# Two-block transformer kernel: sums of squares of the input through a buffer per tile, input scaled by 1/rms ahead of the last modulation columns

## The chip, the cores and the metric

The kernel runs on 1 core of one Trainium2 chip. The metric is the device time of one execution in microseconds; three runs of the kernel before took 3841.53, 3845.0 and 3848.81 us, median 3845.0 us.

## What is computed

The reference is a chain of two diffusion-style blocks (gated linear attention, then neighbourhood attention, each with a convolutional feed-forward part) and two further blocks, all in float32 with D = 1024, 512 latent tokens and 256 context tokens. The change touches only its very beginning: the first normalisation and modulation, whose result `h` goes into the product with `gla_w_in`.

```python
def rms_norm(x, g):
    y = xf * lax.rsqrt(jnp.mean(xf * xf, axis=-1, keepdims=True) + EPS)
    return y * g
def modulate(x, g, shift, scale):
    return rms_norm(x, g) * (1 + scale) + shift

mod_l = silu(c) @ ada_w[0] + ada_b[0]          # 6 parts of 1024; the same for the context with c_ctx
h_l = modulate(x_lat, norm1_g[0], sh1_l, s1_l)
h_c = modulate(x_ctx, norm1_g[0], sh1_c, s1_c)
proj = concat(h_c, h_l) @ gla_w_in[0]
```

## The kernel before, in words

Activations lie transposed, features on the 128 partitions: `X` is 8 tiles (k = 0 to 7) of 768 columns, of which columns 0 to 255 are the context and 256 to 767 the latent tokens (`lat(X, k)`). The products with weights run as three fp32r matmuls (high x high, high x low, low x high): each factor is split in a rounded half (`AH`, `WHI`, written by ScalarE) and the rest (`AL`, `WLO`, written by VectorE). `high_half` (L1375) and `low_half` (L2104) split one 128x1024 piece of weights; three such pieces are held in `RAW`, and SP may load piece i only once the low half of piece i - 3 is made (`weights`, L2990).

Five programs, one for each engine, are written out by hand; every instruction that others need counts up its engine's semaphore under a name (`q.did(name)`), and `q.wait_ge(name)` waits for it. Each engine works through its own list in order. A name of the form `fence("end_norm0")` stands for the end of the start-up in all four compute engines.

The start-up is the part that the change rewrites. It does three things.

1. The modulation columns. The weights `ada_w` come in 512 KB pieces ("side" pieces, L2967), four to a group of 512 outputs; groups 0 to 3 are needed before the first normalisation. Piece m uses one of six slots, so piece m waits until `ada_chunk` of piece m - 6 has run on TensorE (`("amm", m - 6)`). `ada_chunk` (L719) is 8 small float32 matmuls. After four of them VectorE copies the row out (`ada_rows`, L2156), TensorE turns it by 4 tiny matmuls (`ada_turn`, L730) and VectorE adds the bias (`ada_add`, L2161). When group 3 is added, `scale_cols` (L2193) makes the factors (1 + scale) * g, named `acol`.
2. The sums of squares. For each k ScalarE squares the latent part into `SQ[0]` and the context part into `SQ[1]` (L1427); TensorE sums over the partitions by a product with ones into PSUM banks 6 and 7 (`square_sum`, L680). With one buffer each, square k + 1 waits for the sum of tile k. Where the eight pairs of sums stand among the chunks of `ada` is set by the table `STATS0_AT`: from the second chunk of group 1 to the third of group 3.
3. The norm. `norm_two` runs two generators side by side, latent and context. ScalarE's (`norm_high`) waits for the last sum and for `acol`, makes 1/rms with Ln (L1399) and Exp (L1402), and then per tile the rounded half with the shift added (L1411) from the VectorE result `ntr`; VectorE's (`norm_low`) makes `ntr = x * acol * rs` (L2134) and the low half `(ntr + shift) - high` (L2128). After tiles 0 and 1 one piece of weights is split on both engines (`between=(0, 1)`).

TensorE then starts `lin_pair` (L654): the first two 128-column jobs of `gla_w_in` together, tile by tile, 12 matmuls of 384 columns for each k, as the halves of that tile come. After that pair it takes the side piece 16 (`ada_chunk`), which SP may load only after `fence("end_norm0")`, as it may the table `lcs` ahead of it and, since they stand behind in SP's list, the weight pieces from number 3 on. SP's list at the start is: small tables; side 0 to 3; latent tiles 0 to 3 of x (1 MB); side 4, 5; the context (1 MB); side 6, 7; latent tiles 4 to 7 (1 MB); side 8 to 15; weight pieces 0 to 2.

Of the kernel before, what the change touches and what calls it, by code (L numbers as in the profile page):

```python
# [15 lines left out]
D = 1024  # L16
# [291 lines left out]
def build(nc, A, out):  # L308
# [17 lines left out]
    def at(name, shape, dt, off):  # L326
        return nc.alloc_sbuf_tensor_at(name, shape, dt, offset=BASE + int(off))

    def ring(name, n, off, shape=(128, TL), dt=F32):
        size = 4 * int(np.prod(shape[1:]))  # L330
        full = tuple(slice(None) for _ in shape)
        return [at(f"{name}{i}", list(shape), dt, off + size * i)[full] for i in range(n)]
# [63 lines left out]
        return [("modmm", i, cg - 1) if cg else ("modmm", 0, 11)]  # L396

    NORM = [(ring(f"nrs{b}_", 1, oV + 8 * KB * b), ring(f"ntr{b}_", 3, oV + 2 * KB + 8 * KB * b)) for b in range(2)]
    QK = at("gqk", [128, 4, 2, T0], F32, oX0)
    Qt, Kt = QK[:, :, 0, :], QK[:, :, 1, :]  # L400
    Vt = at("gv", [128, 6, D], F32, oV)
# [145 lines left out]
    U = Buf(UH, UL)  # L547
    RL = ring("rl", 3, oX0 + 80 * KB)

    STATS0_AT = ((1, 1), (1, 3), (2, 0), (2, 2), (2, 4), (3, 0), (3, 1), (3, 2))  # L550
    NA_ITEMS = [(j, i) for j in range(8) for i in range(4)]
    KIND = (0, 1, 1, 2)
    MLA_ITEMS = [(j, i) for j in range(4) for i in range(4)]
# [22 lines left out]
    def squares_of(h, s, e_):  # L576

        return SQO[(h, s) == (3, 1)][e_]

    def fence(name):  # L580
        return [(name, n) for n in ("pe", "act", "dve", "pool")]

# [2 lines left out]
    def pe_program(q):  # L585
# [122 lines left out]
        def ada_chunk(i, cg, g):  # L708

            m = next(side_count)  # L710
            b = cg % 2 if m < SIDE_IN else 6
            if g == 0:
                bank(b, ("rows", i, cg))
            p = PS[b]
            q.wait_ge(("aw", m), ("cs",))
            for k in range(2):
                for half in range(2):
                    at32, at2 = 64 * k + 32 * half, 2 * (2 * g + k)
                    mm = e.matmul(p[at32:at32 + 32, 0:256], CS[:, at2:at2 + 32], side_slot(m)[0][:, k, 256 * half:256 * half + 256],  # L719
                                  start=g == 0, stop=g == 3, skip_group_check=True)  # L720
# [12 lines left out]

        def ada(i, cg, mb_bank):
            for g in range(4):
                ada_chunk(i, cg, g)
                yield
            yield
            ada_turn(i, cg, mb_bank)
            yield  # L740

        def ada_beside(fill):

            for n, (i, cg) in enumerate(fill):
# [9 lines left out]
            for _ in range(n):  # L754
                next(side, None)

        k = 0
        for cg in range(4):
            for n, _ in enumerate(ada(0, cg, 2 + cg % 2)):
                if (cg, n) in STATS0_AT:  # L760
                    if k == 0:
                        bank(6, ("ln", "x", 0)), bank(7, ("ln", "x", 1))
                    square_sum("x", k, TL, PS[6], k == 0, k == 7, 0, 0)
                    square_sum("x", k, TC, PS[7], k == 0, k == 7, 1, 1)
                    k += 1
        q.note("end_norm0", "pe")


# [595 lines left out]
    def act_program(q):  # L1364
# [48 lines left out]
                    yield  # L1413
            yield

        def norm_two(N_, stats, i, n, mem, free, between=()):
            gens = [norm_high(N_ + v, stats, r, 8, lambda k, a=a, w=w: AH[:, k, a:a + w], mem[r],
                              free + [("acol", i, n)], bias=lambda k, r=r: mod(i, 3 * n, r, k), rbank=6 + r)
                    for r, (v, (a, w)) in enumerate((("l", SEGL), ("c", SEGC)))]
            for k, _ in enumerate(zip(*gens)):  # L1420
                if k in between:
                    high_half()

        def square(S, k, r, src, buf, *ready):
            q.wait_ge(*ready)
# [34 lines left out]
        e.activation(CS[:, 0:16].rearrange("p (k v) -> p v k", v=2), SMT[:, ca:ca + 16].rearrange("p (v k) -> p v k", v=2),  # L1460
                     ACT.Silu).then_inc(q.did("cs"))

        k = 0
        for cg in range(4):
            for n in range(6):
                if (cg, n) in STATS0_AT:
                    square("x", k, 0, lat(X, k), 0, *sq_by[0], ("x_lat", k // 4))
                    square("x", k, 1, X[:, k, 0:TC], 1, *sq_by[1], ("x_ctx",))
                    sq_by[:] = [[("sqmm", "x", k, 0)], [("sqmm", "x", k, 1)]]
                    k += 1  # L1470
        norm_two("g", "x", 0, 0, NORM, [], (0, 1))
        q.note("end_norm0", "act")


# [620 lines left out]
    def dve_program(q):  # L2095
# [43 lines left out]
            low(srcs - 1)  # L2139
            yield  # L2140

        def norm_two(N_, i, n, mem, free, ready, between=()):
            gens = [norm_low(N_ + v, None, 8, lambda k, a=a, w=w, r=r: (X[:, k, a:a + w], ready(k, r)),
                             lambda k, r=r: ACOL[:, i, n, r, k:k + 1],
                             lambda k, a=a, w=w: AH[:, k, a:a + w], lambda k, a=a, w=w: AL[:, k, a:a + w],
                             mem[r], free + [("acol", i, n)], bias=lambda k, r=r: mod(i, 3 * n, r, k))
                    for r, (v, (a, w)) in enumerate((("l", SEGL), ("c", SEGC)))]
            for k, _ in enumerate(zip(*gens)):
                if k in between:
                    low_half()  # L2150

# [6 lines left out]
        def ada_add(i, cg, b):  # L2158
# [3 lines left out]
                            PS[b][:, 0:8].rearrange("p (j h v) -> p h j v", h=2, v=2),  # L2162
                            SMT[:, ab:ab + 4].rearrange("p (h j) -> p h j", h=2).unsqueeze(3).to_broadcast([128, 2, 2, 2]),
                            ALU.add).then_inc(q.did("mod", i, cg))

        def ada(i, cg, mb_bank):
            for g in range(4):
                yield
            ada_rows(i, cg, cg % 2)
            yield  # L2170
            ada_add(i, cg, mb_bank)
            yield

        def ada_beside(fill):
            for n, (i, cg) in enumerate(fill):
# [20 lines left out]
        for cg in range(4):  # L2196
            for _ in ada(0, cg, 2 + cg % 2):
                pass
        scale_cols(0, 0)
        norm_two("g", 0, 0, NORM, [], lambda k, r: [("x_ctx",)] if r else [("x_lat", k // 4)], (0, 1))  # L2200
        q.note("end_norm0", "dve")


# [658 lines left out]
    def pool_program(q):  # L2862
# [6 lines left out]
                e.tensor_tensor(SQ[0], SQ[0], SQ[1], ALU.add).then_inc(q.did("sqacc", S, k))  # L2869

        e.memset(CS[:, :], 0.0).then_inc(q.did("cs_zero"))
        q.note("end_norm0", "pool")


# [75 lines left out]
    def sp_program(q):  # L2950
# [47 lines left out]
        load(SMT[:, 0:sm["_n"]], A["small"], "small")  # L2998
        load(FIX[:, :], A["fix"], "fix")
        load(SEL[:, :], A["sel"], "sel")  # L3000
        for _ in range(4):
            side()
        load(lat4(X, 0), XT[:, 0:4, :], "x_lat", 0)
        for _ in range(2):
            side()
        load(X[:, :, 0:TC], CTX, "x_ctx")
        for _ in range(2):
            side()
        load(lat4(X, 4), XT[:, 4:8, :], "x_lat", 1)
        for _ in range(8, 16):  # L3010
            side()
        weights(LOOK + 1)
        load(CG[:, :], A["cg"], "cg", after=[("modmm", 0, 2), ("modmm", 0, 3)])
# [174 lines left out]
```

## Time and profile before

| what | value |
|---|---|
| median of three runs | 3845.0 us |
| the profiled execution, its own time | 3843.47 us |
| its span, first to last instruction | 3841.7 us |
| TensorE busy | 97% of the span |
| VectorE, ScalarE, GpSimd busy | 41%, 36%, 6% |
| mean granted TensorE clock | 0.990 |

The page gives busy times over the whole span; the start-up is 2% of it, so it is read from the timeline and from busy times of short stretches instead. All times in those views count from the first instruction of the span.

### The profile page before, as it was taken

How to read it: one execution, taken by the hardware profiler on the slowest of the kernel's cores; microseconds unless marked ns; L12 is line 12 of the kernel's file. 1: busy time of each engine (PE TensorE's matmuls, PEld its weight loads, DVE VectorE, ACT ScalarE, POOL GpSimd, SP SyncE). 2: the span in 40 equal slices, each digit the busy share in tenths (PEclk: the TensorE clock that was granted, in tenths of full speed). 3: DMA queues.
4: the chain of work that ended last, by engine and by line, in shares of the span. 5: the costliest groups of instructions: out<-in, count | busy, mean ns of one | idle time of the engine just before them, and what ended most of it. 6: DMA issues, size and time to landing. Idle time of an engine off the chain costs nothing.

```text
span 3841.7 us, 45535 instructions
## 1 busy us (share of the span) xinstructions
PE 3713.4 (97%) x19200; PEld 2993.6 (78%) x19200; DVE 1590.8 (41%) x2532; ACT 1389.0 (36%) x2257; POOL 233.7 (6%) x191
## 2 busy tenths in 40 slices
PE   7998899999999999999899999999999999999998
PEld 5887777888887977888666768888877676888887
DVE  3216735423434155545445443433334544343333
ACT  3235523212224255323346442342324544234232
POOL 0000010000000001000000001120110001012011
PEclk9999999999999999999999999999999999999999
DMA  6320022333322222233211123322221122332322
GB/s 225 110 88 2 28 83 88 112 122 130 110 64 83 66 69 77 94 93 96 89 57 50 66 72 99 104 93 99 94 93 57 54 71 71 96 105 93 99 93 83
DMA packets 108702, 333.98 MB, mean 87 GB/s; under 512 B 11473, under 2 KB 26705, under 8 KB 108369
## 3 DMA queue, kind: packets, MB, share of 16 engines
q1 hardware_dynamic: 108496, 331.06, 26.7%
q8 instruction: 151, 2.47, 0.3%
q14 instruction: 55, 0.44, 0.0%
HBM read 327.35 MB, written 2.10 MB: 86 GB/s over the span
## 4 chain that ended last, share of the span: by engine, by line
PE 92%; DVE 4%; ACT 2%; DMA 1%; issue 1%; POOL 0%; SPq 0%; DVEq 0%; ACTq 0%
PE ps L618 69%; PE ps L671 6%; PE ps L654 2%; PE ps L719 1%; PE ps L680 1%; PE ps L1213 1%; PE ps L1061 1%; PE ps L1049 1%; PE ps L1040 1%; PE ps L863 1%; PE ps L890 1%; DMA aw<-ada_d 1%; PE ps L1216 1%; PE ps L1092 1%; PE ps L1257 1%
## 5 line engine op out<-in xcount | busy, mean ns | idle before, releaser
L2104 DVE TENSOR_TENSOR wlo<-raw,whi 128x1024 fp32r<-128x1024 f32 (+3 forms) x547 | 618.9, 1132 | 888.2 <-ACT whi L1375 887.2
L1375 ACT ACTIVATE whi<-raw 128x1024 fp32r<-128x1024 f32 (+3 forms) x547 | 527.1, 965 | 795.0 <-PE ps L618 624.9
L618 PE MATMUL ps<-bh,whi 128*128 128x512 f32 x1248 | 494.7, 396 | 0.1
L618 PE MATMUL ps<-bh,wlo 128*128 128x512 f32 x1248 | 486.0, 389 | 0.0
L618 PE MATMUL ps<-bl,whi 128*128 128x512 f32 x1248 | 485.9, 389 | 0.0
L618 PE MATMUL ps<-ah,whi 128*128 128x512 f32 (+2 forms) x1424 | 423.3, 356 | 0.2 <-ACT gv L1500 0.2
L618 PE MATMUL ps<-al,whi 128*128 128x512 f32 (+2 forms) x1424 | 417.7, 352 | 0.0
L618 PE MATMUL ps<-ah,wlo 128*128 128x512 f32 (+2 forms) x1424 | 415.0, 350 | 0.0
L618 PEld LDWEIGHTS ps<-ah,whi 128*128 128x128 f32 x1424 | 240.0, 188 | 51.1 <-issue 18.8
L618 PEld LDWEIGHTS ps<-bh,whi 128*128 128x128 f32 x1248 | 234.2, 188 | 58.1 <-issue 7.6
L618 PEld LDWEIGHTS ps<-bl,whi 128*128 128x128 f32 x1248 | 234.4, 188 | 50.5 <-issue 2.9
L618 PEld LDWEIGHTS ps<-bh,wlo 128*128 128x128 f32 x1248 | 234.2, 188 | 49.3
L618 PEld LDWEIGHTS ps<-ah,wlo 128*128 128x128 f32 x1424 | 242.1, 188 | 31.5
L618 PEld LDWEIGHTS ps<-al,whi 128*128 128x128 f32 x1424 | 241.3, 188 | 29.4
L618 PE MATMUL ps<-uh,whi 128*128 128x512 f32 x512 | 199.2, 389 | 0.0
L618 PE MATMUL ps<-ul,whi 128*128 128x512 f32 x512 | 199.2, 389 | 0.0
L618 PE MATMUL ps<-uh,wlo 128*128 128x512 f32 x512 | 199.2, 389 | 0.0
L2869 POOL TENSOR_TENSOR sq<-sq,sq 128x512 f32<-128x512 f32 x50 | 77.0, 1540 | 1905.8 <-ACT sq L1427 1905.8
L2831 DVE TENSOR_TENSOR ul<-rl,uh 128x512 fp32r<-128x512 f32 x64 | 44.3, 693 | 204.2 <-ACT uh L2061 204.2
L618 PEld LDWEIGHTS ps<-ul,whi 128*128 128x128 f32 x512 | 96.1, 188 | 20.1
L618 PEld LDWEIGHTS ps<-uh,whi 128*128 128x128 f32 x512 | 96.1, 188 | 19.9
L618 PEld LDWEIGHTS ps<-uh,wlo 128*128 128x128 f32 x512 | 96.1, 188 | 19.8
(356 smaller groups left out, 5926.9 us busy)
## 6 DMA issues: line engine op xcount, KB each, us to landing
raw<-weights_d SPq DMA_DIRECT2D x447, 512.0 KB, 3.4
aw<-ada_d SPq DMA_DIRECT2D x96, 512.0 KB, 3.7
raw<-weights_d SPq DMA_DIRECT2D x48, 256.0 KB, 2.6
raw<-weights_d SPq DMA_DIRECT2D x44, 192.0 KB, 2.3
x<-nab_d SPq DMA_DIRECT2D x24, 256.0 KB, 2.8
x<-x_t_d SPq DMA_DIRECT2D x4, 1024.0 KB, 7.4
dt<-rtab_d SPq DMA_DIRECT2D x16, 256.0 KB, 2.8
out_d<-x SPq DMA_DIRECT2D x4, 512.0 KB, 3.1
```

Of the source, the lines that this page charges most:

```text
L618: m = e.matmul(p[:, 0:n], tiles(w, i)[:, k, :], xs[:, x0 + k, c0:c0 + n], start=pi == 0 and k == 0 and ti == 0, stop=i == job and k == kt ...
L654: m = e.matmul(p[:, 0:n], tiles(w, i)[:, k, :], xs[:, k, c0:c0 + n], start=k == 0 and ti == 0, stop=k == 7 and ti == 2, skip_group_check=True)
L671: m = e.matmul(p, xs[:, x0 + 2 * g + k, c0:c0 + 128], tiles(w, i)[:, k, :], start=g == 0 and k == 0 and pi == 0, stop=g == chunks - 1 and ...
L680: e.matmul(p[:, 0:n], ONES, SQ[buf][:, 0:n], start=start, stop=stop, skip_group_check=True).then_inc(q.did("sqmm", S, k, r))
L719: mm = e.matmul(p[at32:at32 + 32, 0:256], CS[:, at2:at2 + 32], side_slot(m)[0][:, k, 256 * half:256 * half + 256], start=g == 0, stop=g == ...
L863: m = e.matmul(p[:, 128 * c:128 * c + 128], XK[l % 2][:, cc], XQ[l % 2][:, cc], start=True, stop=True, skip_group_check=True)
L890: m = e.matmul(p[:, 128 * c:128 * c + 128], l_, r_, start=j == 0, stop=j == len(terms) - 1, skip_group_check=True)
L1040: m = e.matmul(ps[b][:, o:o + 256], NQ[r, j, 128 * i:128 * i + 128], NK[r, j, c0:c0 + 256], start=True, stop=True, skip_group_check=True)
L1375: e.activation(flat(WHI, j), raw(j), ACT.Copy).then_inc(q.did("hi", j))
L2104: e.tensor_tensor(flat(WLO, j), raw(j), flat(WHI, j).bitcast(F32), ALU.subtract).then_inc(q.did("lo", j))
L2831: e.tensor_tensor(UL[:, jj, :], RL[m % 3], UH[:, jj, :].bitcast(F32), ALU.subtract).then_inc(q.did("ul", l, half, jj))
L2869: e.tensor_tensor(SQ[0], SQ[0], SQ[1], ALU.add).then_inc(q.did("sqacc", S, k))
```

## The change

`STATS0_AT`, the generator `ada` and `between` go. The squares get sixteen buffers of their own (`SQX`, in memory that the attention uses later), so ScalarE squares a tile as soon as it has landed, and TensorE's order is written out: chunks of group 0; sums of latent tiles 0 to 3; turn 0; two chunks of group 1; sums of latent tiles 4 to 7; two chunks; the eight sums of the context; turn 1; groups 2 and 3 with turn 2 ahead of the last two chunks. ScalarE makes both 1/rms as soon as their sums are there. VectorE (tiles 0 to 3) and GpSimd (tiles 4 to 7) multiply `X` by 1/rms in place (`input_scaled`). With `acol` there, ScalarE makes the rounded half of the latent part straight from the scaled `X` (Identity with scale and bias, float32 in, fp32r out), and VectorE makes the unrounded value `nt` apart from that (`tensor_scalar`) and subtracts. For the context ScalarE makes `nt` and its rounded copy, and VectorE only subtracts. SP's list is: side 0, 1; latent tiles 0 to 3; side 2, 3; latent tiles 4 to 7; side 4, 5; context; side 6 to 11; weight piece 0; side 12 to 15; weight pieces 1, 2.

```diff
+    SQX = [ring("sqxl", 8, oX0), ring("sqxc", 8, oX0 + 16 * KB, (128, TC))]
-    STATS0_AT = ((1, 1), (1, 3), (2, 0), (2, 2), (2, 4), (3, 0), (3, 1), (3, 2))
+    def input_scaled(e, q, k):
+        for r, v in enumerate("lc"):
+            x, rs = X[:, k, 0:TC] if r else X[:, k, TC:], NORM[r][0][0][:, 0:(TL, TC)[r]]
+            q.wait_ge(("rs", "g" + v), ("x_ctx",) if r else ("x_lat", k // 4), ("sq", "x", k, r))
+            e.tensor_tensor(x, x, rs, ALU.mult).then_inc(q.did("xr", k, r))
 # TensorE
-        for cg in range(4):
-            for n, _ in enumerate(ada(0, cg, 2 + cg % 2)):
-                if (cg, n) in STATS0_AT:
...
+        ada_chunks(0, range(4))
+        input_sums(0, range(4))
+        ada_turn(0, 0, 2)
+        ada_chunks(1, range(2))
+        input_sums(0, range(4, 8))
+        ada_chunks(1, range(2, 4))
+        input_sums(1, range(8))
+        ada_turn(0, 1, 3)
+        ada_chunks(2, range(4))
+        ada_chunks(3, range(2))
+        ada_turn(0, 2, 2)
+        ada_chunks(3, range(2, 4))
+        ada_turn(0, 3, 3)
 # ScalarE
-        norm_two("g", "x", 0, 0, NORM, [], (0, 1))
+        input_squares(0, range(8))
+        input_squares(1, range(8))
+        for r in range(2):
+            input_rms(r)
+        high_half()
+        for k in range(8):
+            q.wait_ge(("xr", k, 0), ("acol", 0, 0))
+            e.activation(lat(AH, k), lat(X, k), ACT.Identity, bias=mod(0, 0, 0, k), scale=ACOL[:, 0, 0, 0, k:k + 1]
+                         ).then_inc(q.did("nh", "gl", k))
+            t = NORM[1][1][k % 3][:, 0:TC]
+            q.wait_ge(("xr", k, 1), *([("nl", "gc", k - 3)] if k >= 3 else []))
+            e.activation(t, X[:, k, 0:TC], ACT.Identity, bias=mod(0, 0, 1, k), scale=ACOL[:, 0, 0, 1, k:k + 1]
+                         ).then_inc(q.did("nt", "gc", k))
+            q.wait_ge(("nt", "gc", k))
+            e.activation(AH[:, k, 0:TC], t, ACT.Copy).then_inc(q.did("nh", "gc", k))
+            if k == 0:
+                high_half()
 # VectorE
-        norm_two("g", 0, 0, NORM, [], lambda k, r: [("x_ctx",)] if r else [("x_lat", k // 4)], (0, 1))
+        def input_low(k):
+            q.wait_ge(("nh", "gl", k), ("nt", "gl", k))
+            e.tensor_tensor(lat(AL, k), NORM[0][1][k % 3], lat(AH, k).bitcast(F32), ALU.subtract).then_inc(q.did("nl", "gl", k))
+            q.wait_ge(("nh", "gc", k))
+            e.tensor_tensor(AL[:, k, 0:TC], NORM[1][1][k % 3][:, 0:TC], AH[:, k, 0:TC].bitcast(F32), ALU.subtract
+                            ).then_inc(q.did("nl", "gc", k))
+        for cg in range(2):
+            ada_rows(0, cg, cg)
+            ada_add(0, cg, 2 + cg)
+        for k in range(4):
+            input_scaled(e, q, k)
+        ada_rows(0, 2, 0)
+        ada_add(0, 2, 2)
+        low_half()
+        ada_rows(0, 3, 1)
+        ada_add(0, 3, 3)
+        scale_cols(0, 0)
+        for k in range(8):
+            q.wait_ge(("xr", k, 0), ("acol", 0, 0), ("mod", 0, 3), *([("nl", "gl", k - 3)] if k >= 3 else []))
+            e.tensor_scalar(NORM[0][1][k % 3], lat(X, k), ACOL[:, 0, 0, 0, k:k + 1], mod(0, 0, 0, k), ALU.mult, ALU.add
+                            ).then_inc(q.did("nt", "gl", k))
+            if k:
+                input_low(k - 1)
+            if k == 1:
+                low_half()
+        input_low(7)
 # GpSimd
         e.memset(CS[:, :], 0.0).then_inc(q.did("cs_zero"))
+        for k in range(4, 8):
+            input_scaled(e, q, k)
 # SP
-        for _ in range(4):
+        for _ in range(2):
             side()
         load(lat4(X, 0), XT[:, 0:4, :], "x_lat", 0)
         for _ in range(2):
             side()
-        load(X[:, :, 0:TC], CTX, "x_ctx")
+        load(lat4(X, 4), XT[:, 4:8, :], "x_lat", 1)
         for _ in range(2):
             side()
-        load(lat4(X, 4), XT[:, 4:8, :], "x_lat", 1)
-        for _ in range(8, 16):
+        load(X[:, :, 0:TC], CTX, "x_ctx")
+        for _ in range(6):
+            side()
+        weights(1)
+        for _ in range(4):
             side()
         weights(LOOK + 1)
```

## Rows read from the trace of the kernel before

**Rows 1.** The page's TensorE busy tenths, the span in 40 slices of 96 us
```profile
PE   7998899999999999999899999999999999999998
```
**Rows 2.** Stretches: length; busy (count) PE, PEld, DVE, ACT, POOL; granted clock; DMA; GB/s
```profile
20.00:30.00 10.00, 9.59 (x58) 3.91 (x57) 0.59 (x2) 2.37 (x7) 0.00 (x0) 1.00 1.04 403
30.00:40.00 10.00, 9.46 (x62) 4.10 (x60) 1.01 (x3) 4.97 (x9) 0.00 (x0) 1.00 0.71 281
...
50.00:60.00 10.00, 7.82 (x29) 7.39 (x29) 8.87 (x17) 5.62 (x9) 0.00 (x0) 0.59 0.01 2
```
**Rows 3.** Timeline, 10 to 40 us: start, length, engine, line, out<-in, count [idle <-releaser]
```profile
10.83 1.08 PE L719 MATMUL ps<-aw,cs 128*32 128x256 f32 x8 [0.23 <-DMA aw<-ada_d]
...
17.09 2.08 PE L680 MATMUL ps<-sq,fix 128*128 128x512 f32 x2
...
25.64 0.64 PE L719 MATMUL ps<-aw,cs 128*32 128x256 f32 x8 [0.41 <-DMA aw<-ada_d]
...
27.70 1.14 PE L719 MATMUL ps<-aw,cs 128*32 128x256 f32 x16
...
32.22 0.50 PE L730 MATMUL ps<-sel,rows 128*128 128x4 f32 x4
...
35.28 1.56 PE L680 MATMUL ps<-sq,fix 128*128 128x512 f32 x4
36.44 0.94 ACT L1427 ACTIVATE sq<-x 128x512 f32<-128x512 f32 x2 [1.12 <-PE ps L680]
...
36.77 0.64 PE L719 MATMUL ps<-aw,cs 128*32 128x256 f32 x8
```
**Rows 4.** Timeline, from the last modulation group to the first projection matmul
```profile
39.53 0.42 DVE L2156 COPY rows<-ps 128x256 f32<-128x256 f32 x1 [6.60 <-PE ps L719]
...
40.86 0.24 DVE L2193 SCALAR_TENSOR_TENSOR acol<-mod,small 128x8 f32<-128x8 f32 x2
...
48.00 1.23 DVE L2104 TENSOR_TENSOR wlo<-raw,whi 128x1024 fp32r<-128x1024 f32 x1 [0.86 <-ACT whi L1375]
...
48.02 1.01 PE L654 MATMUL ps<-ah,whi 128*128 128x384 f32 x2 [7.41 <-ACT whi L1375]
```
**Rows 5.** Timeline of the pair of projections: two consecutive job steps
```profile
60.42 0.51 PE L654 MATMUL ps<-ah,whi 128*128 128x384 f32 x2
...
61.46 0.51 PE L654 MATMUL ps<-ah,whi 128*128 128x384 f32 x2
```
**Rows 6.** Timeline, the end of the start-up and what follows it
```profile
63.80 1.54 DVE L2128 SCALAR_TENSOR_TENSOR al<-ntr,mod,ah 128x256 fp32r<-128x256 f32 x3
...
65.42 0.33 SPq L2958 DMA_DIRECT2D lcs<-lc_d  x1
...
70.47 0.51 PE L654 MATMUL ps<-ah,wlo 128*128 128x384 f32 x2
...
72.34 0.64 PE L719 MATMUL ps<-aw,cs 128*32 128x256 f32 x8 [1.36 <-DMA aw<-ada_d]
```
**Rows 7.** Groups by line and shape, whole span: xcount | busy us, mean ns
```profile
L2510 DVE TENSOR_SCALAR np<-np,tiny 128x512 f32<-128x512 f32 x64 | 28.3, 484 | 1.1
L2840 DVE TENSOR_TENSOR x<-x,utmp 128x512 f32<-128x512 f32 x32 | 22.2, 692 | 1.1
L2104 DVE TENSOR_TENSOR wlo<-raw,whi 128x256 fp32r<-128x256 f32 x8 | 3.4, 422 | 4.1 <-ACT whi L1375 4.1
...
L2879 POOL TENSOR_TENSOR gqk<-gqk,cg 128x512 f32<-128x512 f32 x8 | 10.3, 1289 | 134.3 <-PE ps L776 134.3
...
L1411 ACT ACTIVATE ah<-ntr,mod 128x512 fp32r<-128x512 f32 x8 | 5.7, 726 | 6.9 <-DVE ntr L2134 6.9
L1411 ACT ACTIVATE ah<-ntr,mod 128x256 fp32r<-128x256 f32 x8 | 4.0, 510 | 2.5 <-DVE ntr L2134 2.5
```
**Rows 8.** Busy time by stretch of 1 us, where the granted clock changes
```profile
44.00:45.00 1.00, 0.00 (x0) 0.00 (x0) 0.75 (x1) 1.00 (x3) 0.00 (x0) 0.76 0.87 345
...
58.00:59.00 1.00, 1.00 (x6) 1.00 (x6) 1.00 (x2) 0.45 (x2) 0.00 (x0) 0.91 0.06 16
```

More of the change, by code:

```diff
@@ L732, in ada_turn @@
             m.then_inc(q.did("modmm", i, cg))
[L734 to L740, printed above, removed]
         def ada_beside(fill):
@@ L755, in beside, with input_sums, ada_chunks @@
                 next(side, None)
-        k = 0
-        for cg in range(4):
-            for n, _ in enumerate(ada(0, cg, 2 + cg % 2)):
-                if (cg, n) in STATS0_AT:
[L761 to L765, printed above, removed]
+        def input_sums(r, ks):
+            p, n = PS[6 + r], (TL, TC)[r]
+            for k in ks:
+                if k == 0:
+                    bank(6 + r, ("ln", "x", r))
+                q.wait_ge(("sq", "x", k, r), ("fix",))
+                e.matmul(p[:, 0:n], ONES, SQX[r][k], start=k == 0, stop=k == 7, skip_group_check=True
+                         ).then_inc(q.did("sqmm", "x", k, r))
+        def ada_chunks(cg, gs):
+            for g in gs:
+                ada_chunk(0, cg, g)
+        ada_chunks(0, range(4))
[11 more added lines that the diff above has]
+        ada_turn(0, 3, 3)
         q.note("end_norm0", "pe")
@@ L1414, in norm_high, with norm_two @@
             yield
-        def norm_two(N_, stats, i, n, mem, free, between=()):
+        def norm_two(N_, stats, i, n, mem, free):
             gens = [norm_high(N_ + v, stats, r, 8, lambda k, a=a, w=w: AH[:, k, a:a + w], mem[r],
@@ L1419, in norm_two @@
                     for r, (v, (a, w)) in enumerate((("l", SEGL), ("c", SEGC)))]
-            for k, _ in enumerate(zip(*gens)):
-                if k in between:
-                    high_half()
+            for _ in zip(*gens):
+                pass
         def square(S, k, r, src, buf, *ready):
@@ L1461, in act_program, with input_squares, input_rms @@
                      ACT.Silu).then_inc(q.did("cs"))
[L1463 to L1470, printed above, removed]
-        norm_two("g", "x", 0, 0, NORM, [], (0, 1))
+        def input_squares(r, ks):
+            for k in ks:
+                q.wait_ge(*([("x_ctx",)] if r else [("x_lat", k // 4)]))
+                e.activation(SQX[r][k], X[:, k, 0:TC] if r else lat(X, k), ACT.Square).then_inc(q.did("sq", "x", k, r))
+        def input_rms(r):
+            rs = NORM[r][0][0][:, 0:(TL, TC)[r]]
+            ln_exp()
+            q.wait_ge(("sqmm", "x", 7, r), ("small",))
+            e.activation(rs, PS[6 + r][:, 0:(TL, TC)[r]], ACT.Ln, scale=1.0 / D, bias=col("eps")).then_inc(q.did("ln", "x", r))
+            q.wait_ge(("ln", "x", r))
+            e.activation(rs, rs, ACT.Exp, scale=-0.5).then_inc(q.did("rs", "g" + "lc"[r]))
+        input_squares(0, range(8))
[13 more added lines that the diff above has]
+            e.activation(AH[:, k, 0:TC], t, ACT.Copy).then_inc(q.did("nh", "gc", k))
+            if k == 0:
+                high_half()
         q.note("end_norm0", "act")
@@ L2140, in norm_low, with norm_two @@
             yield
-        def norm_two(N_, i, n, mem, free, ready, between=()):
+        def norm_two(N_, i, n, mem, free, ready):
             gens = [norm_low(N_ + v, None, 8, lambda k, a=a, w=w, r=r: (X[:, k, a:a + w], ready(k, r)),
@@ L2147, in norm_two @@
                     for r, (v, (a, w)) in enumerate((("l", SEGL), ("c", SEGC)))]
-            for k, _ in enumerate(zip(*gens)):
-                if k in between:
-                    low_half()
+            for _ in zip(*gens):
+                pass
         def ada_rows(i, cg, b):
@@ L2164, in ada_add @@
                             ALU.add).then_inc(q.did("mod", i, cg))
[L2166 to L2172, printed above, removed]
         def ada_beside(fill):
@@ L2194, in scale_cols @@
                                        ALU.add, ALU.mult).then_inc(q.did("acol", i, n))
-        for cg in range(4):
-            for _ in ada(0, cg, 2 + cg % 2):
-                pass
-        scale_cols(0, 0)
-        norm_two("g", 0, 0, NORM, [], lambda k, r: [("x_ctx",)] if r else [("x_lat", k // 4)], (0, 1))
+        def input_low(k):
[14 more added lines that the diff above has]
+        ada_add(0, 3, 3)
+        scale_cols(0, 0)
+        for k in range(8):
[7 more added lines that the diff above has]
+        input_low(7)
         q.note("end_norm0", "dve")
```

## The prediction

> **What bounds the kernel now.** I read first the page's slices: TensorE is busy nine tenths or more in most of the 40 slices, and the first slice is among the low ones [rows 1]. The change edits only what lies before about 65 us, so everything behind must gain or lose as a block; the question is how many microseconds earlier TensorE enters the work that keeps it full. The busy times by stretch say what limits each part of the start-up. From 20 to 40 us TensorE is busy 9.5 of every 10 us, with the DMA at 403 GB/s in the first of these stretches [rows 2]: there the chunks of modulation weights and the sums of squares fill TensorE, and the timeline shows them back to back [rows 3]. ScalarE does wait for TensorE with each pair of squares (1.12 us, [rows 3]), but that is not TensorE waiting for ScalarE. So the single square buffers cost almost nothing after 25.6 us. Before that TensorE waits for modulation weights from the DMA (0.41 us at 25.64, [rows 3]) and runs slowly: a sum of 512 columns takes 2.08 us at 17.09, while a sum of 512 and one of 256 columns together take 36.77 - 35.28 = 1.49 us later [rows 3].
>
> Then comes the hole. `acol` is ready at 40.86 + 0.24 = 41.1 us; the first projection matmul starts at 48.02, after 7.41 us of idle TensorE [rows 4]. Between lie Ln, Exp, the product with acol and rs, the rounded half, all in a row, twice over. The granted clock falls to half at about 44.5 us and is back at full only at about 58.1 [rows 8], so the pair of projections runs at half speed for most of its first 10 us (mean 0.59 from 50 to 60, [rows 2]). The pair ends at 71.0, and TensorE then waits 1.36 us for side piece 16, at 72.34 [rows 6]. SP issues that load behind the fence, once VectorE has made its last low half at 63.80 + 1.54 = 65.34: the table goes out at 65.42 and the piece is there 6.92 us later [rows 6]. So the wait that ends last is the fence, 24.2 us behind `acol`, plus 7.0 us of transfer.
>
> **The change, part by part.** Two numbers decide: A, when `acol` is ready (now 41.1), and the distance from A to the fence (now 24.2).
>
> A first. The removed waits on the square buffers give nothing by themselves, as said; what moves is the order. Latent tiles 0 to 3 land two side pieces earlier, so chunk 3, which starts at 10.83 [rows 3], is put back by 1 MB at 0.4 MB/us, 2.6 us less the gap in the old order: I take its end as 14.0. From there TensorE has its work at hand. Until turn 1 these are 4 chunks at 0.57 (two took 1.14, [rows 3]) = 2.3, the eight pairs of sums at 1.49 = 11.9, and two turns at 0.45 (the matmuls take 0.50, overlapping what follows, [rows 3]) = 0.9: 15.1 us at full speed. At half speed every microsecond yields half. In the trace TensorE became fast between 22.7 and 25.6 us after a stretch with gaps, and the second time after some 5.6 us without a gap (52.5 to 58.1, [rows 8]). Now it is without a gap from 14.0, so I put the change at 20: 3.0 us lost, turn 1 ends at 32.1. Bounds: fast from 17 (A 1.5 us earlier), or only from 24 as now (A 2 us later).
>
> VectorE adds the bias of group 1 at 32.3 and then scales four tiles: 0.69 for 512 columns and 0.42 for 256 [rows 7], 4.4 us, to 36.7. Behind this wait stands the row copy of group 2, 0.42, and with it turn 2 on TensorE and the last two chunks, queued behind turn 2. This is a wait that the change adds. TensorE has done six more chunks (3.4 us) by 35.5 and stands idle until 37.2. Turn 2 0.45, two chunks 1.14: 38.8. VectorE meanwhile makes a low half (1.23, [rows 4]) behind the bias of group 2, to 39.1, then copy 0.42, turn 0.50, bias 0.17 and scale_cols 0.26: A = 40.5. The side pieces fit: piece 15 may load once chunk 9 is done at about 33.2, and with 1 MB ahead of it at 0.4 MB/us plus about 1.7 us to land it is there at about 37.2, before its chunk. GpSimd's eight products, 1.29 us for 512 columns [rows 7] and about 0.7 for 256, run from 29 to about 41; tile 4 is wanted only at A + 7.6. The 1/rms are made by 33. So A = 40.5, with bounds 38.5 and 43: between a small gain and a small loss, near the old value because TensorE's work in the start-up is the same.
>
> From A to the fence. ScalarE makes the latent high half (0.73), the context `nt` (0.51) and its copy (about 0.42): A + 1.65. VectorE, which made the latent `nt` beside that, subtracts the context by A + 2.1, and TensorE starts there, not at A + 6.9. ScalarE splits weight piece 1 until A + 2.7, VectorE its low half until A + 3.95, and each further tile costs VectorE 0.48 + 0.69 + 0.42 = 1.59 [rows 7] (before: two operations more in kind, 2.1 us a tile) and ScalarE 0.73 + 0.51 + 0.42 = 1.66 less overlap [rows 7]. VectorE ends at A + 3.95 + 6 x 1.59 + 1.11 = A + 14.6; ScalarE at A + 2.7 + 7 x 1.63 = A + 14.1. `tensor_scalar` at 0.48 is from the nearest row; at the 0.69 of a two-input operation the fence is at A + 16. Fence A + 14.6 = 55.1, 10.2 us earlier than 65.3. Side piece 16 comes 7.0 us behind it as now: 62.1 against 72.3.
>
> TensorE's pair: a job step is 61.46 - 60.42 = 1.04 us at full clock [rows 5], two per tile. The first tile ends at about A + 4.3 behind the low half, the second can start at A + 5.5, and seven tiles at 2.08 end at A + 20.1, ahead of the piece at A + 21.6. The idle stretch before is about 2.5 us instead of 7.4. If the clock falls there all the same and comes back 5.6 us behind A + 5.5, the pair ends at about A + 23.1, which is then what is last: 1.5 us less gain. Weight pieces 1 and 2, now issued behind piece 15, land by 40.5: in time.
>
> The sum: 72.3 - 62.1 = 10.2 us. Against the profiled execution's 3843.5 that is 3833.3; the median of the runs is 1.5 us higher than that execution, so 3834.8.
>
> **A rule against the rows.** GpSimd and VectorE multiply tiles at the same time, which no row of the old start-up shows. The Trainium skill ("GPSIMD Engine Reference", "Key points") says that GpSimd shares its SBUF interfaces with VectorE and contends with VectorE instructions that have two SBUF inputs, which `tensor_tensor` on X and 1/rms is. By that rule the scaling would stretch and push A; by the row of 0.69 us it would not. For the clock, the Trainium skill ("TensorE: Matmul & The Clock Gate", "What's actually happening") calls the throttled state the default, which activity releases; that would favour the earlier release taken above, and no run yet shows it for the new order.
>
> **The rivals.**
>
> *The start-up eats the gain (part of it).* Mechanism: the row copy of group 2 stands behind VectorE's four scalings, and those behind TensorE's context sums. If TensorE is fast only from 24 us, A is 42.4; if the scalings take half as long again beside GpSimd, 2.2 us more; if the pair starts at half clock, 1.5 us. For it: the added queue is on the path from 32 to 37 us by my own sum. Against it: TensorE has no gaps before. Any two together leave a gain of 5 to 7 us: 3838 to 3840, within 0.2%.
>
> *More than forecast.* TensorE fast from 17 us and sums of squares closer packed than in pairs (the two kinds no longer alternate): A = 38.6, gain 12 to 14 us, about 3832.
>
> *Slower.* Mechanism: TensorE does not leave the half clock during the start-up, because the sums in one long queue wait for x, and stays there in the pair. Then until turn 1 it needs 30 us instead of 18, A = 53, and the pair at 4.2 us a tile ends near A + 35 = 88 against 72.3: 16 us slower, 3861. It turns into a loss once the clock rises later than about 40 us. Against it: the old order reached full speed with more gaps than the new one has.
>
> *The change does not do what it says.* The fence might be hidden if TensorE were not waiting for the piece behind it. But 1.36 us of wait [rows 6] shows that piece and pair end close together, and the pair starts earlier too; with the fence free of charge the gain would be that of the pair, 9 to 11 us. It makes no other time.
>
> **How the numbers follow.** Forecast 3834.8, its own range 3832 to 3837: chance 0.60. More than forecast, 3829 to 3832: 0.12. Gain partly eaten, 3837 to 3842: 0.25. Slower, 3848 and more: 0.03. The three runs of before lie 7 us apart, so the median itself may sit 1.5 us off; the range that holds 8 in 10 is 3829.5 to 3841. A measurement of this kernel can tell 0.2%, 7.7 us, from no change: faster than 3837.3 has 0.72, within it 0.25, slower than 3852.7 0.03.
>
> **What would show it.** In the changed profile: no wait of ScalarE for TensorE between squares; sums of squares at full speed from about 20 us; TensorE idle about 2 us at 35 to 37 behind VectorE's copy; `acol` at 40.5; first projection matmul at about 42.6; the table `lcs` issued at about 55 and the side chunk at about 62; the rest of the span equal. The forecast is wrong if `acol` comes after 43, if VectorE needs more than 1.8 us a tile in the loop, or if a later stretch gives back what the first gave.

## The result, and the profile after

The changed kernel takes 3839.72 us (median of 22 runs, 3837.31 to 3848.09), the kernel before in the same sessions 3847.0 (22 runs, 3841.53 to 3855.74). The ratio is 0.9981, with a 95% interval from 0.9974 to 0.9987: 7.3 us less, between 5.0 and 10.0. The forecast was 3834.8, a gain of 10.2; the measured time lies in the range given (3829.5 to 3841.0), but a gain of 0.19% is just below the 0.2% that was called faster, in the case named "the start-up eats the gain (part of it)". The forecast was added up from a median of 3845.0 of three runs; over 22 runs that kernel has 3847.0, so 2 us of the gain of 7.3 lie in what it is compared with. (For some of the later versions the ratio is not the quotient of the medians beside it; the ratio with its interval is what counts.)

The landmarks of the start-up, from the two timelines (us from the start of the span):

| | before | forecast | after |
|---|---|---|---|
| turn 1 done | - | 32.1 | 29.9 |
| VectorE's four tiles scaled | - | 36.7 | 39.2 |
| `acol` ready (A) | 41.1 | 40.5 | 44.5 |
| first projection matmul | 48.0 | 42.6 | 46.9 |
| table `lcs` issued (end of the fence) | 65.4 | 55.1 | 59.4 |
| side chunk behind the pair | 72.3 | 62.1 | 66.7 |

So of 10.2 us forecast for the last landmark 5.6 came. The timeline of the changed kernel, VectorE and GpSimd on the scalings and what follows, in place of [rows 4]:

```profile
29.96 0.17 DVE L2197 TENSOR_TENSOR mod<-ps,small 128x8 f32<-128x8 f32 x1 [3.54 <-PE ps L737]
30.04 9.19 DVE L586 TENSOR_TENSOR x<-x,nrs 128x512 f32<-128x512 f32 x8
39.16 0.41 DVE L2192 COPY rows<-ps 128x256 f32<-128x256 f32 x1
...
44.30 0.24 DVE L2221 SCALAR_TENSOR_TENSOR acol<-mod,small 128x8 f32<-128x8 f32 x2
```
```profile
30.62 8.33 POOL L586 TENSOR_TENSOR x<-x,nrs 128x256 f32<-128x256 f32 x7 [2.48 <-ACT nrs L1490]
```

The eight products of VectorE last 9.19 us, not 4.4, and GpSimd works on its own from 30.6 us on beside them. By shape, between 30 and 39.2 us (busy us, mean ns):

```profile
L586 DVE TENSOR_TENSOR x<-x,nrs 128x512 f32<-128x512 f32 x4 | 5.9, 1484 | 0.0
L586 POOL TENSOR_TENSOR x<-x,nrs 128x512 f32<-128x512 f32 x3 | 4.3, 1442 | 0.0
L586 POOL TENSOR_TENSOR x<-x,nrs 128x256 f32<-128x256 f32 x4 | 4.2, 1059 | 2.5 <-ACT nrs L1490 2.5
L586 DVE TENSOR_TENSOR x<-x,nrs 128x256 f32<-128x256 f32 x4 | 3.8, 949 | 0.0
```

The mean of 1484 ns hides two values: the first product of 512 columns began before GpSimd's resumed and took 0.69 us, the other three took 1.74 to 1.76.

TensorE in the same stretch, in place of [rows 3], and the end of the pair, in place of [rows 6]:

```profile
14.31 5.64 PE L763 MATMUL ps<-sqxl,fix 128*128 128x512 f32 x8
...
21.23 3.70 PE L763 MATMUL ps<-sqxl,fix 128*128 128x512 f32 x8
...
33.73 0.64 PE L726 MATMUL ps<-aw,cs 128*32 128x256 f32 x8 [0.62 <-DMA aw<-ada_d]
39.62 1.01 PE L737 MATMUL ps<-sel,rows 128*128 128x4 f32 x4 [5.25 <-DVE rows L2192]
40.57 1.94 PE L726 MATMUL ps<-aw,cs 128*32 128x256 f32 x16
...
46.94 0.98 PE L661 MATMUL ps<-ah,whi 128*128 128x384 f32 x2 [2.88 <-DVE al L2228]
...
66.73 0.64 PE L726 MATMUL ps<-aw,cs 128*32 128x256 f32 x8 [0.40 <-DMA aw<-ada_d]
```

The second four sums take 3.70 us where the first took 5.64: TensorE became fast while it worked on the first, at about 18 us by the starts of its matmuls. This is read from durations; the granted clock shows 1.00 there, over the slow matmuls too, as it does in the old start-up. After 31.8 TensorE has caught up with the side pieces and waits for two of them, 0.69 and 0.62 us. Then it waits 5.25 us for VectorE's copy, and when it comes back two chunks take 1.94 us, at about half the speed. The granted clock (last but two) by stretch of 1 us:

```profile
17.00:18.00 1.00, 1.00 (x3) 0.45 (x2) 0.00 (x0) 1.00 (x3) 0.00 (x0) 1.00 1.00 370
...
34.00:35.00 1.00, 0.37 (x8) 0.00 (x0) 1.00 (x2) 0.00 (x0) 1.00 (x1) 1.00 1.06 406
35.00:36.00 1.00, 0.00 (x0) 0.00 (x0) 1.00 (x2) 0.00 (x0) 1.00 (x2) 0.66 0.99 401
36.00:37.00 1.00, 0.00 (x0) 0.00 (x0) 1.00 (x2) 0.00 (x0) 1.00 (x2) 0.50 1.03 418
...
52.00:53.00 1.00, 1.00 (x7) 1.00 (x6) 1.00 (x3) 1.00 (x3) 0.00 (x0) 0.80 0.00 0
```

The clock falls from its upper to its lower level (2.4 to 1.2 GHz) at about 35.3, 1 us into the long wait, and is back at about 52.4.

### The profile page after: what moved, and what is told of

It is laid out like the page before. It is cut to its first block, busy times and chain, and to the rows that moved or that the text cites. A ratio compares the mean times of both kernels' runs of the same rounds, so it can differ in the third digit from the quotient of the medians.

```text
span 3839.0 us, 45566 instructions
## 1 busy us (share of the span) xinstructions
PE 3713.3 (97%) x19200; PEld 2998.7 (78%) x19200; DVE 1594.2 (42%) x2532; ACT 1389.4 (36%) x2265; POOL 243.1 (6%) x199
## 4 chain that ended last, share of the span: by engine, by line
PE 93%; DVE 4%; ACT 2%; issue 1%; DMA 0%; POOL 0%; SPq 0%; DVEq 0%; ACTq 0%
PE ps L625 69%; PE ps L678 6%; PE ps L661 2%; PE ps L726 1%; PE ps L1230 1%; PE ps L880 1%; PE ps L1078 1%; PE ps L1066 1%; PE ps L1057 1%; PE ps L687 1%; PE ps L907 1%; PE ps L1233 1%; PE ps L1109 1%; PE ps L1274 1%; PE ps L1151 1%
```

## The experiments

Two theories stood after the result. *Contention*: VectorE and GpSimd slow each other, that makes the products late, and the row copy behind them makes `acol` late. *The queue*: the copy would be late behind any four tiles; the place is what counts. Beside them, open points of the prediction: what the order is worth alone, what the buffers are, and whether the fall of the clock or the transfer behind the fence ends last. Four profiles share the early part of the changed kernel (its own two, and those of the fillers and of the later table in it); in them `acol` came at 44.5, 43.6, 43.8 and 43.3, so the first profile, against which the distances below are given, is the latest, and a microsecond of each is scatter.

**GpSimd waits until VectorE is done.**

```diff
+        q.wait_ge(("xr", 3, 1))
         for k in range(4, 8):
             input_scaled(e, q, k)
```

> The changed kernel, with one wait added: GpSimd starts its four tiles only when VectorE has scaled its last one, so the two never multiply at the same time during VectorE's part. Theory 'contention' (the two engines slow each other on two-input operations: in the changed kernel VectorE's 512-column products took 1.48 us on average where 0.69 was expected): VectorE's eight products take 4.4 us instead of 9.2, acol is ready at about 40 instead of 44.5, and the side chunk behind the pair starts at about 62 instead of 66.7. Rival 'slow operands' (the product with 1/rms in place is slow by itself): eight products still take 9 us, acol stays at 44.5 and the chunk at 66.7, or later if GpSimd's tiles come too late.

VectorE's rows in this kernel, and GpSimd's:

```profile
30.14 3.84 DVE L586 TENSOR_TENSOR x<-x,nrs 128x512 f32<-128x512 f32 x8
...
35.22 1.22 DVE L2141 TENSOR_TENSOR wlo<-raw,whi 128x1024 fp32r<-128x1024 f32 x1
...
39.32 0.92 DVE L2221 SCALAR_TENSOR_TENSOR acol<-mod,small 128x8 f32<-128x8 f32 x2
40.27 2.24 DVE L2244 TENSOR_SCALAR ntr<-x,acol,mod 128x512 f32<-128x512 f32 x2
42.44 1.21 DVE L2226 TENSOR_TENSOR al<-ntr,ah 128x512 fp32r<-128x512 f32 x1
```
```profile
34.06 9.04 POOL L586 TENSOR_TENSOR x<-x,nrs 128x512 f32<-128x512 f32 x8 [33.19 <-DVE x L586]
```

The same eight products take 3.84 us when GpSimd is silent: contention is shown, the slow operands are ruled out. `acol` is ready at 40.2 and the side chunk starts at 63.19, 3.5 us earlier than in the first profile of the changed kernel. That is 1 us later than expected, because the contention moved: GpSimd is now at work from 34 to 43, and two `tensor_scalar` take 2.24 us instead of 1.00, the factors of `acol` 0.92 instead of 0.24. The weight low half at 35.22 kept its 1.22 us; here GpSimd paid. The low half had begun first, and the product of 256 columns that GpSimd began beside it took 1.73 us, where 0.72 is what it takes with VectorE silent:

```profile
L586 POOL TENSOR_TENSOR x<-x,nrs 128x256 f32<-128x256 f32 x1 | 1.7, 1734 | 0.0
```

The same stands in the kernel before, at 1499 us: the low half takes its usual time, and a GpSimd square that begins in the middle of it takes 1.81 us where others take 1.28 to 1.30:

```profile
1498.67 1.23 DVE L2104 TENSOR_TENSOR wlo<-raw,whi 128x1024 fp32r<-128x1024 f32 x1 [0.40 <-ACT whi L1375]
1499.23 1.81 POOL L2869 TENSOR_TENSOR sq<-sq,sq 128x512 f32<-128x512 f32 x1 [267.86 <-ACT sq L1427]
```

In both places the operation that began later was the longer one, by about the time that the earlier one had left.

The clock fell here too, at about 35.4, behind waits of 0.78 and 0.62 us for side pieces and with no long wait for VectorE. Median of 10 runs 3837.04, ratio to before 0.9982 (0.9972 to 0.9992). The intervals of this ratio and of the changed kernel's 0.9981 overlap: the earlier chunk is seen in the profile, a gain in the total is not shown.

**The row copy first.**

```diff
-        for k in range(4):
-            input_scaled(e, q, k)
-        ada_rows(0, 2, 0)
+        input_scaled(e, q, 0)
+        ada_rows(0, 2, 0)
+        for k in range(1, 4):
+            input_scaled(e, q, k)
```

> The changed kernel, with VectorE's row copy of group 2 moved ahead of three of its four scaled tiles, so that turn 2 and the last two chunks don't wait behind them. If contention alone makes acol late, little changes: the products still end at about 39.6 and the low half at 40.8, acol comes at about 43, the side chunk at about 65.2. Rival 'the queue' (the copy standing behind the products is what counts): acol at 40 or before and the side chunk at 62.

`acol` was ready at 41.0 (40.76 + 0.24) and the side chunk at 63.09, one run 3837.62. The products are as slow as before (six in 6.67 us), yet the chunk comes 3.6 us earlier. That is more than the 1.5 expected if contention alone counted, and near the 62 of the rival, though `acol` missed the rival's 40: the queue is as much a part of the loss as the contention. The two are links of one chain, slow products in front of a copy that TensorE waits for, and taking away either frees most of it. The gains don't add: the kernel with all products on VectorE, below, takes away both and has the chunk 1.2 us earlier still, not 3.5.

**The order alone.** New loads, buffers, chunks and sums; the norm of before.

```diff
-        for r in range(2):
-            input_rms(r)
...
+        norm_two("g", "x", 0, 0, NORM, [], (0, 1))
```

> One part of the change alone: the sixteen square buffers and the new order of loads, chunks and sums, with the norm of the kernel before (1/rms made after acol, product with acol and rs on VectorE). If the order is what the start-up needs, acol comes at about 38.6, held only by the last side piece (landed at about 36.3), 2.5 us before the 41.1 of the kernel before, and the distance from acol to the end of the start-up stays 24.2: side chunk at 69.8, 2.5 us gained. If the order gives nothing, acol is at 41 and the chunk at 72.3.

Its `acol` and side chunk:

```profile
39.95 0.24 DVE L2201 SCALAR_TENSOR_TENSOR acol<-mod,small 128x8 f32<-128x8 f32 x2
```
```profile
36.21 1.94 PE L726 MATMUL ps<-aw,cs 128*32 128x256 f32 x16
71.34 0.64 PE L726 MATMUL ps<-aw,cs 128*32 128x256 f32 x8 [1.19 <-DMA aw<-ada_d]
```

`acol` at 40.2 and the chunk at 71.34: 1.0 us gained at that mark instead of 2.5, because TensorE had caught up with the loads (it waited 1.92 and 0.64 us for two side pieces), the clock fell at about 33.6, and the turn and the last two chunks ran at half clock (1.94 us for the two). The distance from `acol` to the chunk is 31.15 us, as before (31.24). Median of 10 runs 3848.04, ratio 1.0001 (0.9992 to 1.0011). The order alone gives no gain in the total; it comes only with the new norm. The new norm in the old order was not run.

**The sixteen buffers alone,** in the old order.

```diff
-                    square_sum("x", k, TL, PS[6], k == 0, k == 7, 0, 0)
-                    square_sum("x", k, TC, PS[7], k == 0, k == 7, 1, 1)
+                    for r, n in enumerate((TL, TC)):
+                        q.wait_ge(("sq", "x", k, r), ("fix",))
+                        e.matmul(PS[6 + r][:, 0:n], ONES, SQX[r][k], start=k == 0, stop=k == 7, ...)
...
```

> The kernel before with the sixteen square buffers alone, everything else in its old order. Prediction's step: the single buffers cost almost nothing, since TensorE is full from 25.6 us; acol at 41.1 within 0.7 us, side chunk at 72.3 within 0.7. Rival: TensorE's order was held by the squares, then acol comes 2 us earlier or more.

`acol` at 41.0, chunk at 72.06: 0.1 and 0.3 us earlier. One run, 3845.21, within those of the kernel before. So the single buffers cost next to nothing in the old order, as predicted.

**All products on VectorE.**

```diff
+        for k in range(4):
+            input_scaled(e, q, k, 0)
         ada_add(0, 1, 3)
+        for k in range(4):
+            input_scaled(e, q, k, 1)
         ada_rows(0, 2, 0)
+        for k in range(4, 7):
+            input_scaled(e, q, k, 0)
         ada_add(0, 2, 2)
         low_half()
+        input_scaled(e, q, 7, 0)
         ada_rows(0, 3, 1)
+        for k in range(4, 6):
+            input_scaled(e, q, k, 1)
...
+            if k in (2, 3):
+                input_scaled(e, q, 4 + k, 1)
...
-        for k in range(4, 8):
-            input_scaled(e, q, k)
```

> The changed kernel with all sixteen products on VectorE and none on GpSimd: the latent products of tiles 0 to 3 before the bias of group 1, row copy 2 right behind the context products of those tiles, tiles 4 to 6 latent behind it, the last two context products inside the loop. 'Contention' theory: each product takes 0.69 or 0.42 us at most, the row copies come as soon as their chunks, acol is held only by the last side piece (36.5) and comes at about 38.7; pair starts at about 41.5, side chunk at about 60.5 to 61, 6 us before the changed kernel's 66.7. Rival 'too much on VectorE': acol at 41, the loop goes at 2.1 us a tile, chunk at 64 or later.

```profile
26.71 2.50 DVE L586 TENSOR_TENSOR x<-x,nrs 128x512 f32<-128x512 f32 x4 [1.16 <-ACT nrs L1490]
29.70 1.43 DVE L586 TENSOR_TENSOR x<-x,nrs 128x256 f32<-128x256 f32 x4 [0.42 <-ACT nrs L1490]
31.38 1.88 DVE L586 TENSOR_TENSOR x<-x,nrs 128x512 f32<-128x512 f32 x3
```

One engine does sixteen products in 8.1 us of its time, less than it needed for eight beside GpSimd. `acol` at 40.1 (38.7 expected; TensorE waited 1.92 and 0.63 us for side pieces, the clock fell at about 33.7, and the turns and the last chunks ran at half clock), chunk at 61.89, 4.8 us before the changed kernel's first profile and 3.8 before its second. Median of 11 runs 3836.6, ratio 0.9976 (0.9967 to 0.9985), an interval that still overlaps with that of the changed kernel.

**The same, with the table behind the side pieces.** SP's list: side 16, 17, weight piece 3, then `lcs`.

```diff
-        load(LCS[:, :], A["lc"], "lc_raw", after=fence("end_norm0"))
+        weights(LOOK + 2)
+        load(LCS[:, :], A["lc"], "lc_raw", after=fence("end_norm0"))
```

> The kernel with all products on VectorE, and in SP's list the table lcs (1.15 MB) moved behind side pieces 16 and 17 and weight piece 3. If the transfer behind the fence is what ends last in that kernel, side piece 16 comes 2.9 us earlier (1.15 MB at 0.4 MB/us) and the chunk follows the pair, at about 59 to 60; if the pair at half clock ends last, nothing moves against the same kernel without the reordering.

The chunk starts at 61.32 without waiting for a load: 21.5 us behind `acol` instead of 21.8. The transfer was hidden behind the pair but for 0.3 us, and the pair, at half clock in its first part, ends last. Median of 8 runs 3836.99, ratio 0.9975 (0.9964 to 0.9985).

**Filler matmuls in the changed kernel,** meant to keep the clock up; what they compute is not used.

```diff
         ada_chunks(3, range(2))
+        for _ in range(10):
+            e.matmul(PS[4][:, 0:256], ONES, FIX[:, 0:256], start=True, stop=True, skip_group_check=True)
         ada_turn(0, 2, 2)
         ada_chunks(3, range(2, 4))
         ada_turn(0, 3, 3)
+        for _ in range(6):
+            e.matmul(PS[4][:, 0:256], ONES, FIX[:, 0:256], start=True, stop=True, skip_group_check=True)
```

> The changed kernel with 16 matmuls of 256 columns into an unused bank, of no use for the result: 10 where TensorE stands idle behind chunk 13 (34.4 to 39.6 us) and 6 behind the last turn. If idleness is what lowers the clock, it stays at full and the pair of projections starts at full speed: steps of 1.04 us a job from the first on, pair over by about 64 instead of 66.3; the side chunk stays at 66.3 to 66.7, since it waits for its load behind the fence. Rival (the clock is what ended last): chunk at 64.

```profile
46.18 0.59 PE L661 MATMUL ps<-ah,whi 128*128 128x384 f32 x2 [0.18 <-DVE al L2232]
65.74 0.64 PE L726 MATMUL ps<-aw,cs 128*32 128x256 f32 x8 [1.66 <-DMA aw<-ada_d]
```
```profile
34.00:35.00 1.00, 1.00 (x10) 0.50 (x3) 1.00 (x1) 0.00 (x0) 1.00 (x2) 0.67 1.01 401
35.00:36.00 1.00, 1.00 (x4) 0.82 (x3) 1.00 (x3) 0.00 (x0) 1.00 (x2) 0.50 1.02 406
...
37.00:38.00 1.00, 1.00 (x4) 0.80 (x4) 1.00 (x2) 0.00 (x0) 1.00 (x2) 0.63 0.09 37
```

The clock did not stay up, though that was expected: it fell at about 34.3, as the first fillers began, behind waits of 1.51 and 0.64 us for side pieces, and came back at about 37.7, under the fillers. So the long wait for VectorE is not what lowers it; in the changed kernel that wait keeps it low. The pair runs at full clock from its start (0.59 for two matmuls instead of 0.98), and TensorE then waits 1.66 us for the load: 22.0 us from `acol` to the chunk, against 22.2. In the changed kernel the slow clock of the pair is covered by the transfer. One run, 3839.94.

**The table later in the changed kernel.** The same edit of SP's list.

> The changed kernel with the table lcs moved behind side pieces 16, 17 and weight piece 3 in SP's list. In the changed kernel the side chunk waited 0.40 us for its load, with the pair over at 66.3; so the chunk moves to 66.3 and no further. If the load was the real bound of the pair too, it moves to 64.

The chunk comes at 64.50, but `acol` came at 43.3 in this execution; from `acol` to the chunk it is 21.2 us instead of 22.2, and TensorE no longer waits for the load. Pair and load end within a microsecond of each other. One run, 3838.55.

**Both, on the kernel with all products on VectorE.** 11 fillers in the gaps of TensorE.

```diff
         ada_chunks(2, range(4))
+        (3 fillers)
-        ada_chunks(3, range(2))
+        ada_chunks(3, range(1))
+        (1 filler)
+        ada_chunks(3, range(1, 2))
         ada_turn(0, 2, 2)
         ada_chunks(3, range(2, 4))
+        (2 fillers)
         ada_turn(0, 3, 3)
+        (5 fillers)
```

> All products on VectorE, lcs later, and 11 filler matmuls of 256 columns into an unused bank (3 behind group 2, 1 between chunks 12 and 13, 2 ahead of the last turn, 5 behind it; of no use for the result). In the same kernel without them the pair began at 42.25 at half clock and the side chunk, which no longer waited for its load, started at 61.3. If the clock of the pair is what ends last there, the pair now runs at full clock from its start and the chunk comes at 59.3 to 59.8; if the fall of the clock can't be held off so, or the load ends last, it stays at 61.

```profile
41.56 0.58 PE L661 MATMUL ps<-ah,whi 128*128 128x384 f32 x2 [0.62 <-DVE al L2237]
```
```profile
59.38 0.64 PE L726 MATMUL ps<-aw,cs 128*32 128x256 f32 x8
```

These fillers stand earlier, from 30.8 us on, between the waits for side pieces, and here the clock did stay up: 1.00 over the whole of 28 to 45 us. With load and products out of the way the clock is what ended last: the chunk at 59.38, 20.2 us behind `acol` instead of 21.5, 13 us before the kernel before. Median of 6 runs 3833.29 (3830.08 to 3839.12), ratio 0.9971 (0.9959 to 0.9982). It has the lowest median of all versions here; its interval overlaps with those of the two versions before it.

**The changed kernel again,** unaltered, beside the last one.

> The changed kernel itself, beside the others on the same chip, for two open points: how much its start-up varies between executions (side chunk at 66.7 in its first profile; the three kernels that share its early part had acol between 43.3 and 44.5), and whether the 132.8 us from gmask to the second load of x, 3.3 more than in the kernel before, belong to the change or to the execution. If to the change, they come again at 132.8 within 0.3; if to where the clock falls, they may be 129.5 as well. Ratio to the kernel before 0.998.

Side chunk at 65.71, `acol` at 43.6, median of 11 runs 3839.99, ratio 0.9985 (0.9976 to 0.9994). The start-up varies by about a microsecond from one execution to the next. From `gmask` to the second load of x it took 130.9 us, where the first profile had 132.8 and the kernel before 129.5: the difference is not the change's own. Against this kernel the version with fillers is 6.7 us faster by the medians of the same session; five of its six runs lie below the fastest of the eleven here.

**The rest of the span.** All landmarks above are of the first 72 us, and the span of the profiled execution fell by only 2.7 us where the chunk came 5.6 earlier. What lies behind the chunk does the same work in every kernel; it took 3769.4 us before, 3772.3 and 3771.6 in the two profiles of the changed kernel, and between 3768.9 and 3775.8 in all. The granted clock of a stretch at 360 us, before and after:

```profile
360.00:370.00 10.00, 6.36 (x43) 5.95 (x42) 7.95 (x14) 6.23 (x13) 0.00 (x0) 0.94 0.01 2
```
```profile
360.00:370.00 10.00, 6.38 (x28) 5.91 (x27) 5.96 (x10) 5.09 (x9) 0.00 (x0) 0.66 0.01 2
```

At the same busy time TensorE does 28 matmuls instead of 43. Summed over stretches of 10 us behind 70 us (each counts 20 us times what its mean clock lacks to 1, since the lower level is half), TensorE was at its lower level for 58 us before, for 68 and 69 in the changed kernel, and for 82 in the kernel where GpSimd waits, which has the longest rest. The kernel with the shortest rest had 66, so the sum doesn't explain each one; that the rest is longer on average with an earlier start is not shown by these single profiles.

## Why the prediction was right, and where it was not

*What bounds the start-up, and that the buffers cost nothing:* right (the kernel with the buffers alone). *Fence and load end last behind the pair, not `acol`'s own chain:* right. From `acol` to the fence 14.6 us were forecast and 59.27 - 44.54 = 14.7 came; from the fence to the chunk 7.0 and 7.5. This part carried 9.6 us of the 10.2, and 31.24 - 22.19 = 9.05 us of it came. The terms in it were less good than their sum: ScalarE needed 0.80 and 0.59 us for its activations with scale and bias, where 0.73 and 0.51 were taken, and 1.65 a tile, near the 1.63 forecast, since they overlap; VectorE needed 1.40 a tile of its own where I had 1.59. At that pace it would have been done at about A + 13.5 (an estimate, 3.95 + 6 x 1.40 + 1.11); it came at A + 14.7 because from about 54 us on it waited for ScalarE, 0.16 to 0.28 us at a time, and went at its 1.65:

```profile
57.91 0.69 DVE L2226 TENSOR_TENSOR al<-ntr,ah 128x512 fp32r<-128x512 f32 x1 [0.28 <-ACT ah L1499]
```

I had VectorE as the engine that ends last there. That the sum came out within 0.1 us is in part luck.

*`acol` at 40.5:* wrong, it came at 44.5 (43.6 the second time), outside its bounds of 38.5 to 43, and `acol` after 43 is a sign that the prediction itself named for being wrong. Three terms:

- TensorE until turn 1, done at 29.9 instead of 32.1: this gave 2.2 us. About half of it is speed: taken as fast from 20 us on, it was fast from about 18, and the first four sums took 5.48 us until the next work began, the second four 3.63: 1.85 us lost, where 3.0 were taken. The rest is that sums and chunks are closer packed than the 1.49 a pair of sums and 0.57 a chunk of the old order: at full speed 13.8 us of work instead of 15.1, less 0.3 for a chunk 3 that ended later than taken (14.3). The rival "more than forecast" named this. By the Trainium skill ("TensorE: Matmul & The Clock Gate", "What's actually happening") activity releases the throttle, and the trace agrees: the start with fewer gaps was fast from about 18 us, the old one from about 24. The speed is read from durations, since the granted clock shows 1.00 in both.
- The four tiles on VectorE: 9.2 us instead of 4.4, which took 4.8. This is the step that failed. I priced the products by rows in which GpSimd was idle, named the contention as a rule of the Trainium skill ("GPSIMD Engine Reference", "Key points"), and gave it half as long again; it was twice as long. The trace agrees with the rule for these products and gives it its size: 1.75 us for 512 columns where GpSimd is at work all the while, 0.69 where it is not.
- The clock behind it: I saw the idle time of TensorE from 35.5 to 37.2, and let the turn and the chunks behind it run at full clock. They ran at half clock, and from the last scaled tile to `acol` it took 5.3 us instead of 3.8. The long idle time is not what lowered the clock: it fell between 33 and 36 in every version with the new order but the one with 11 fillers, also in those where TensorE did not wait for VectorE there. What those falls have in common is that TensorE had caught up with the loads and waited for side pieces of group 3, which the prediction left out (it had six chunks in a row, done by 35.5; they were done at 34.4, waits included). The long wait kept the clock low.

-2.2 + 4.8 + 1.5 = +4.1, against the 4.0 us by which `acol` was late in the first profile.

*Pair at A + 20.1, or 23.1 at half clock:* it ended at about A + 21.8, between the two; the experiment with fillers shows that the clock there was hidden, but for 0.2 us. *The rivals:* the one that came true is the first, with its place (the copy behind the scalings) and too small a price. The slower rival had the clock right as a danger but in the wrong place: TensorE reached full speed in the long queue of sums, and the clock fell behind them, at the waits for side pieces. *The size:* at the chunk 5.6 and 6.6 us were gained in two profiles, and 7.3 by the medians; these agree within the interval. The rest of the span was to be equal; in the two profiles it was 2.9 and 2.2 us longer, which the prediction had as a sign of being wrong and which single profiles can't tell from scatter. That the median lies in the range is owed to the range's width: it reached to a start-up that eats part of the gain, and `acol` was 4 us late.

## What to carry to other kernels

A part of the work given to GpSimd beside VectorE must be priced by a run in which both are busy with SBUF operands; here one engine alone did sixteen products faster than two did them together. Ask what is queued behind a step on its engine: a copy of 0.42 us behind a slow batch held TensorE for 5.25 us. And where a transfer and a slow clock end within a microsecond of each other, each is worth little until the other is gone: between `acol` and the chunk the fillers alone brought 0.2 us, the table alone 1.0, and the fillers 1.3 once the table was out of the way (21.5 to 20.2). These are single profiles.

## What the runs showed of the hardware

A float32 `tensor_tensor` of 512 columns in SBUF takes VectorE 0.69 us alone and 1.74 to 1.76 beside GpSimd doing the same; GpSimd takes 1.27 alone and 1.44 on average beside it. `tensor_scalar`, with one tensor input, suffered too (2.24 us for two, instead of 1.00), and so did instructions of 8 columns (0.92 instead of 0.24 for two); a weight low half of 1024 columns that had begun ahead of GpSimd's product took 1.22 us, as ever, and the product of 256 columns beside it 1.73 instead of 0.72. Sixteen small matmuls into an unused bank, in TensorE's gaps of 5 and 3 us, did not keep its clock from falling to 1.2 GHz at 34.3 us, but brought it back to 2.4 at 37.7, ahead of the pair; eleven that began at 30.8, between the waits for side pieces, kept it at 2.4 GHz until the pair and through it (mean granted clock 1.00 from 28 to 45 us).
